# In every attention loop, the turn of a head's probabilities is issued last on TensorE, and VectorE copies the turned head before it takes the maxima

## The chip, the cores and the metric

The kernel runs on one core of a Trainium2 chip. The metric is the time of one execution on the device, in microseconds (us), taken as the median of the runs. PE or TensorE is the matmul engine, DVE or VectorE and ACT or ScalarE the two elementwise engines, SP the engine that issues the weight loads.

## What is computed

Two small transformer stages on 256 tokens of width 1024, batch 1, all in float32. The first block joins a gated linear recurrence with a three-branch attention (compressed, selected and window keys, 16 query heads on 4 key heads) and a gated feed-forward layer. The second has two layers, each an attention and a feed-forward layer: a rotary causal attention of 16 heads, and a latent attention (MLA) of 16 heads. What bears on the change is the same in all:

```python
s = jnp.einsum("bqhd,bkhd->bhqk", qi, k, preferred_element_type=jnp.float32) * scale
s = jnp.where(key_pos[None, :] <= qpos[:, None], s, NEG_INF)
p = jax.nn.softmax(s, axis=-1).astype(v.dtype)
return jnp.einsum("bhqk,bkhd->bqhd", p, v)
```

With 256 tokens the selected branch and the window branch of the first attention are both plain causal attention, so its loop runs over 32 heads (16 query heads in each of two branches), and the other two loops over 16.

## The kernel before, in words

The weights are cut in 128x1024 chunks, which go through one stream: SP loads a chunk into one of three raw buffers, ACT writes its rounded part (`split_high`, L1088, into `w_high`), DVE the rest (`split_low`, L1486, into `w_low`), and TensorE multiplies high by high, high by low and low by high (`split_product`, L531 to L537). The ring of split chunks has six places. A product of 128 outputs over a width of 1024 is 24 matmuls.

Each engine runs a program of its own, written out in order, and waits on semaphores. An attention is a loop with the same index i on three engines; head i is begun in iteration i and finished in iteration i + 3 (count + 3 iterations in all).

- TensorE, `attention` at L635. `scores(i)` (L638) makes the products of queries and keys of head i in one of three banks and adds the mask (matmuls at L644, L645, L647). `turn(i)` (L651) transposes the probabilities of head i, three 128x128 blocks, into a bank (L657). `values(i)` (L661) multiplies them with the values (L669, L670, L671); it waits until DVE has copied the turned head to SBUF. `between(i)` makes products that don't belong to this head: in the first attention half a merge gate, 12 matmuls (`merge_between`, L921; iterations 0, 1, 4 to 19, 32 and 34), in the second the turn of a rotary operand (`turn_rope`, L961, matmul at L968) and the 24 matmuls of the next query or key tile (`next_query_or_key`, L980; up to iteration 11, the turn up to 12), in the third the 9 matmuls of the query of head i + 3 (`query_product`, L1044; up to iteration 12).
- ACT, `attention` at L1153: two exponentials a head with their sums (L1161, L1163), then further work: a `split_high`, in the second attention the copy of a product (`rope_operand`, L1384), in the third the copy of a query (`query_copy`, L1445).
- DVE, `attention` at L1553. In iteration i: `before(i)` (first attention: `merge_scaled`, L1857, which reads the merge gate's bank; the next gate's first half waits for it, L882), `row_max(i)` (L1556: two reductions), `copy_turned` (L1562), every fourth iteration `output(g)` (L1568: one over the sums, and the scaled output of four heads, L1573 to L1585; in iterations 6, 10, 14, ... it waits for `values` of the same iteration of TensorE), and `after(i)`: in the first attention a `split_low`, in the second `rope(i + 3)` with a `split_low` (L1940), in the third `query_rope(i + 3)` (L2012; it reads the bank of the query product, and the product of the next head waits for it, L1050) and in six iterations a `split_low`.

The turned heads have two banks in the first and third attention and one in the second (L440, L441); their copies in SBUF have two places. After the loop `turn_output` (L686, matmuls at L696) turns the outputs, and ACT and DVE split them (`output_high`, `output_low`) for the projection. Its last pair of tiles waits for the last `output`.

Of the kernel before, what the change touches and what calls it, by code (L numbers as in the profile page):

```python
# [147 lines left out]
def build(nc, weight_stream, small_in, x_in, out):  # L148
    with ExitStack() as ctx:
# [293 lines left out]
        def of(banks, i):  # L443
            return bank[banks[i % len(banks)]]
# [83 lines left out]
        def _(pe):  # L528
# [106 lines left out]
            def attention(n, count, q, kpad, v, probs, probs_t, banks_free, before=None, between=None, use=ALL_BANKS):  # L635
                done = NH * n

                def scores(i):  # L638
                    if before:
                        before(i)  # L640
                    if i >= 3:
                        pe.wait_ge(probs_ready, done + i - 2)
                    b = of(use.scores, i)
                    mm(b[:, 0:P], q(i, 0), kpad(i)[:, 0:P], start=True, stop=False, skip_group_check=True)  # L644
                    mm(b[:, P:3 * P], q(i, 1), kpad(i), start=False, stop=False, skip_group_check=True)  # L645

                    mm(b[:, :].rearrange("p (a c) -> p a c", c=2 * P)[:, :, 0:P], ident_b[:, :],  # L647
                       mask_b[:, :].unsqueeze(1).to_broadcast([P, 2, P]), start=False, stop=True,
                       skip_group_check=True).then_inc(scores_ready, 1)

                def turn(i):  # L651
                    pe.wait_ge(probs_ready, done + i + 1)
                    ring = len(use.turned)
                    if i >= ring:
                        pe.wait_ge(probs_copied, done + i - ring + 1)
                    for j in range(3):
                        ins = nc.tensor.transpose(of(use.turned, i)[:, j * P:(j + 1) * P],  # L657
                                                  probs[:, i % 3, j * P:(j + 1) * P], ident)
                    ins.then_inc(probs_turned, 1)

                def values(i):  # L661
                    pe.wait_ge(probs_copied, done + i + 1)
                    g = i // 4
                    if i % 4 == 0 and g >= 2:
                        pe.wait_ge(o_read, 4 * n + g - 1)
                    b = of(use.outputs, g)
                    pt = probs_t[:, i % 2, :]
                    at = (i % 4) * HD
                    mm(b[:, at:at + HD], pt[:, 0:P], v(i, 0), start=True, stop=True)  # L669
                    mm(b[:, S + at:S + at + HD], pt[:, P:2 * P], v(i, 0), start=True, stop=False)  # L670
                    mm(b[:, S + at:S + at + HD], pt[:, 2 * P:3 * P], v(i, 1), start=False,  # L671
                       stop=True).then_inc(pv_done, 1)

                for i in range(count + 3):
                    if i < count:
                        scores(i)
                    if i == 2:
                        banks_free()
                    if 2 <= i < count + 2:
                        turn(i - 2)  # L680
                    if i >= 3:
                        values(i - 3)
                    if between:
                        between(i)

            def turn_output(n, o):  # L686

# [233 lines left out]
            def merge_between(i):  # L921

                if i in MG_AT:
                    at = MG_AT.index(i)
                    merge_gates(MG_EARLY + at // 2, (at % 2,))

            attention(0, 2 * NH, lambda i, t: q0[:, i % NH // 2, t * P:(t + 1) * P],
                      lambda i: k0[:, i // NH, i % 2, i % NH // 4, :],
                      lambda i, t: v0[:, i // NH, t, (i % NH // 4) * HD:(i % NH // 4 + 1) * HD], probs0, probs_t0,
# [58 lines left out]
            for n in range(1, QK_AHEAD):  # L988
                query_or_key(n)
                turn_rope(n - 1)  # L990
            pe.wait_ge(zeros_ready, 2)
            attention(2, NH, lambda h, t: q1[:, h // 2, t * P:(t + 1) * P], lambda h: k1[:, h % 2, h // 2, :],
                      lambda h, t: v1[:, t, h * HD:(h + 1) * HD], probs1, probs_t1, lambda: None,
                      lambda h: pe.wait_ge(rope_done, max(2 * (h // 2) + 2, h + 1)), next_query_or_key, SIX_BANKS)
# [77 lines left out]
            for h in range(UQ_AHEAD):  # L1072
                query_product(h)
            attention(3, NH, lambda h, t: q2[:, h, t * P:(t + 1) * P], lambda h: k2[:, h, :],
                      lambda h, t: v2[:, t, h * HD:(h + 1) * HD], probs2, probs_t2,
                      lambda: None,
# [396 lines left out]
        def _(dve):  # L1473
# [9 lines left out]
            def link(ins):  # L1483
                dve.wait_ge(dve_step, mark(ins))
# [68 lines left out]
            def attention(n, count, o, probs_t, gated=False, before=None, after=None, use=ALL_BANKS):  # L1553
                done = NH * n

                def row_max(i):  # L1556
                    dve.wait_ge(scores_ready, done + i + 1)
                    b, h = of(use.scores, i), i % NH
                    v.tensor_reduce(neg_max[:, h, 0:1], b[:, 0:P], AX.X, ALU.max, negate=True)  # L1559
                    v.tensor_reduce(neg_max[:, h, 1:2], b[:, P:3 * P], AX.X, ALU.max, negate=True).then_inc(max_ready, 1)  # L1560

                def copy_turned(i):  # L1562
                    dve.wait_ge(probs_turned, done + i + 1)
                    if i >= 2:
                        dve.wait_ge(pv_done, done + i - 1)
                    v.tensor_copy(probs_t[:, i % 2, :], of(use.turned, i)[:, 0:3 * P]).then_inc(probs_copied, 1)  # L1566

                def output(g):  # L1568

                    dve.wait_ge(pv_done, done + 4 * g + 4)  # L1570
                    heads = slice(4 * g % NH, 4 * g % NH + 4)
                    w = weights_o[:, :, heads]
                    link(v.reciprocal(w, sums[:, :, heads]))  # L1573
                    if gated:
                        link(v.tensor_tensor(w, w, nsa_gate[:, :, heads, 1 + 4 * g // NH], ALU.mult))
                    dst = o[:, :, heads, :]
                    src = of(use.outputs, g)[:, :].rearrange("p (t h d) -> p t h d", t=TT, h=4)
                    wide = w.unsqueeze(3).to_broadcast([P, TT, 4, HD])
                    if gated:
                        if 4 * g >= NH:  # L1580
                            dve.wait_ge(o_read, g - 3)
                        link(v.tensor_tensor(o_part, src, wide, ALU.mult))
                        v.tensor_tensor(dst, dst, o_part, ALU.add).then_inc(o_read, 1)
                    else:
                        v.tensor_tensor(dst, src, wide, ALU.mult).then_inc(o_read, 1)  # L1585

                for i in range(count + 3):
                    if before:
                        before(i)
                    if i < count:  # L1590
                        row_max(i)
                    if 2 <= i < count + 2:
                        copy_turned(i - 2)
                    if i >= 3 and i % 4 == 2:
                        output((i - 3) // 4)
                    if after:
                        after(i)
# [307 lines left out]
            def merge_split(i):  # L1905
                if i - 1 in MG_LATE:
                    split_low(BASE["mg"] + MG_LATE[i - 1] + RING)

            attention(0, 2 * NH, o0, probs_t0, gated=True, before=merge_gate, after=merge_split)
            merge_gate(2 * NH + 3)  # L1910
            output_low(0)
# [43 lines left out]
            for n in range(QK_AHEAD - 1):  # L1955
                rope(n)
            attention(2, NH, o1, probs_t1,
                      after=lambda i: rope(i + QK_AHEAD - 1) if i + QK_AHEAD <= SIZE["qk1"] else None, use=SIX_BANKS)
            output_low(1)
# [65 lines left out]
            def behind_maxima(i):  # L2025
                query_rope(i + UQ_AHEAD)
                query_split(i + UQ_AHEAD - 2)

            attention(3, NH, o2, probs_t2, after=behind_maxima)
            output_low(2)  # L2030
            stage("wo2", lambda i: None, count=DT - LATE)
# [188 lines left out]
```

## Time and profile before, and how to read them

| | us |
|---|---|
| median of 3 runs | 1224.09 |
| lowest and highest run | 1222.18, 1225.47 |
| the profiled execution | 1222.21 |
| its span | 1220.4 |
| TensorE busy in it | 1162.5 (95%) |
| DVE busy | 915.0 (75%) |
| ACT busy | 681.7 (56%) |
| mean granted clock of TensorE | 0.982 |

The span is the time from the first to the last instruction in the trace; the execution's own time lies 1.8 us above it. Times in the trace count from the span's start. A row of a timeline gives the start, the duration, engine, line, operation, output and inputs, the shape and how many instructions are merged; in square brackets stand the idle time before it and what ended it. Matmuls overlap, so what a matmul costs is read from start to start. The granted clock is 1.00 where TensorE runs at 2.4 GHz and 0.50 at 1.2 GHz.

The three attention loops lie at 262 to 347 us (head scores of iteration 20 at 319.68), at 632 to 702 us (iteration 12 at 689.43) and at 957 to 1001 us (iteration 13 at 990.94).

### The profile page before, as it was taken

How to read it: one execution, taken by the hardware profiler on the slowest of the kernel's cores; microseconds unless marked ns; L12 is line 12 of the kernel's file. 1: busy time of each engine (PE TensorE's matmuls, PEld its weight loads, DVE VectorE, ACT ScalarE, POOL GpSimd, SP SyncE). 2: the span in 40 equal slices, each digit the busy share in tenths (PEclk: the TensorE clock that was granted, in tenths of full speed). 3: DMA queues.
4: the chain of work that ended last, by engine and by line, in shares of the span. 5: the costliest groups of instructions: out<-in, count | busy, mean ns of one | idle time of the engine just before them, and what ended most of it. 6: DMA issues, size and time to landing. Idle time of an engine off the chain costs nothing.

```text
span 1220.4 us, 25342 instructions
## 1 busy us (share of the span) xinstructions
PE 1162.5 (95%) x9633; PEld 1132.0 (93%) x9633; DVE 915.0 (75%) x1579; ACT 681.7 (56%) x1184; POOL 9.2 (1%) x12
## 2 busy tenths in 40 slices
PE   5987998999999999999999999999998899999996
PEld 5987898999999999999899899999997899999996
DVE  6778789467777899888867758777776776777775
ACT  5755774334454666565654455655565745655552
POOL 1000000000000100000000000000000000000000
PEclk9988998999999999999999999999999999999998
DMA  6564444432216477666463325766654224576660
GB/s 222 189 209 131 147 156 130 147 121 71 70 53 190 137 224 215 200 189 192 149 194 111 98 87 193 223 194 196 192 156 149 93 70 132 187 220 201 190 190 35
DMA packets 52780, 190.82 MB, mean 156 GB/s; under 512 B 5984, under 2 KB 5984, under 8 KB 52704
## 3 DMA queue, kind: packets, MB, share of 16 engines
q1 hardware_dynamic: 52416, 188.77, 49.8%
q8 instruction: 54, 0.88, 0.3%
q10 hardware_dynamic: 288, 0.99, 0.2%
q14 instruction: 22, 0.18, 0.0%
HBM read 188.69 MB, written 1.05 MB: 155 GB/s over the span
## 4 chain that ended last, share of the span: by engine, by line
PE 82%; DVE 8%; ACT 5%; issue 2%; DMA 2%; SPq 0%; DVEq 0%; ACTq 0%
PE bank L535 23%; PE bank L537 23%; PE bank L536 23%; DVE w_low L1491 2%; DMA w_raw<-weight_stream 2%; PE bank L645 2%; ACT w_high L1096 2%; PE bank L657 1%; PE bank L671 1%; PE bank L670 1%; PE bank L644 1%; PE bank L669 1%; PE bank L543 1%; PE bank L545 1%; PE bank L544 1%
## 5 line engine op out<-in xcount | busy, mean ns | idle before, releaser
L1491 DVE TENSOR_TENSOR w_low<-w_raw,w_high 128x1024 fp32r<-128x1024 f32 x356 | 434.3, 1223 | 153.5 <-ACT w_high L1096 151.4
L1096 ACT ACTIVATE w_high<-w_raw 128x1024 fp32r<-128x1024 f32 x356 | 375.4, 1059 | 289.3 <-PE bank L537 217.9
L535 PE MATMUL bank<-h_high,w_high 128*128 128x256 f32 x1824 | 518.2, 284 | 14.7 <-DVE h_low L1529 9.7
L536 PE MATMUL bank<-h_low,w_high 128*128 128x256 f32 x1824 | 509.3, 279 | 0.0
L537 PE MATMUL bank<-h_high,w_low 128*128 128x256 f32 x1824 | 509.0, 279 | 0.0
L535 PEld LDWEIGHTS bank<-h_high,w_high 128*128 128x128 f32 x1824 | 347.0, 190 | 17.6 <-issue 12.9
L536 PEld LDWEIGHTS bank<-h_low,w_high 128*128 128x128 f32 x1824 | 347.3, 190 | 0.5
L537 PEld LDWEIGHTS bank<-h_high,w_low 128*128 128x128 f32 x1824 | 346.9, 190 | 0.0
L535 PE MATMUL bank<-r_high,w_high 128*128 128x256 f32 x878 | 248.6, 283 | 12.8 <-ACT arena L1297 7.3
L536 PE MATMUL bank<-r_low,w_high 128*128 128x256 f32 x878 | 245.4, 280 | 0.0
L537 PE MATMUL bank<-r_high,w_low 128*128 128x256 f32 x878 | 245.4, 279 | 0.0
L535 PEld LDWEIGHTS bank<-r_high,w_high 128*128 128x128 f32 x878 | 167.3, 191 | 16.9 <-ACT arena L1297 8.4
L536 PEld LDWEIGHTS bank<-r_low,w_high 128*128 128x128 f32 x878 | 167.3, 190 | 0.1
L537 PEld LDWEIGHTS bank<-r_high,w_low 128*128 128x128 f32 x878 | 167.0, 190 | 0.0
L1613 DVE SCALAR_TENSOR_TENSOR arena<-arena,small 128x255 f32<-128x255 f32 (+1 forms) x184 | 87.8, 477 | 5.7 <-ACT arena L1189 2.4
L1161 ACT ACTIVATE arena<-bank,stats 128x128 f32<-128x128 f32 x64 | 23.5, 367 | 63.3 <-DVE stats L1560 61.7
L1189 ACT ACTIVATE arena<-arena,small 128x256 f32<-128x256 f32 x68 | 40.0, 589 | 12.9 <-DVE arena L1627 12.8
L1515 DVE TENSOR_TENSOR r_low<-arena,r_high 128x256 fp32r<-128x256 f32 (+1 forms) x91 | 39.7, 437 | 5.0 <-ACT r_high L1202 4.0
L1627 DVE TENSOR_TENSOR arena<-bank,rstd 128x256 f32<-128x256 f32 x68 | 28.7, 423 | 18.1 <-PE bank L537 18.0
L1559 DVE TENSOR_REDUCE stats<-bank 128x1 f32<-128x128 f32 x64 | 18.5, 289 | 29.5 <-PE bank L647 29.2
L1566 DVE COPY arena<-bank 128x384 f32<-128x384 f32 x64 | 34.9, 548 | 4.7 <-PE bank L657 4.7
L645 PE MATMUL bank<-arena 128*128 128x256 f32 x128 | 38.3, 381 | 0.0
(205 smaller groups left out, 1164.4 us busy)
## 6 DMA issues: line engine op xcount, KB each, us to landing
w_raw<-weight_stream SPq DMA_DIRECT2D x356, 512.0 KB, 3.7
x<-x_in SPq DMA_DIRECT2D x4, 256.0 KB, 6.0
out<-arena SPq DMA_DIRECT2D x4, 256.0 KB, 2.3
small<-small_in ACTq DMA_DIRECT2D x1, 937.5 KB, 8.4
small<-small_in ACTq DMA_DIRECT2D x1, 30.0 KB, 4.0
```

The lines of the kernel that those rows point to most:

```text
L535: mm(out_ap, wh, high, start=start, stop=False, skip_group_check=True)
L536: mm(out_ap, wh, low, start=False, stop=False, skip_group_check=True)
L537: return mm(out_ap, wl, high, start=False, stop=stop, skip_group_check=True)
L645: mm(b[:, P:3 * P], q(i, 1), kpad(i), start=False, stop=False, skip_group_check=True)
L1096: fn(w_high[:, c % RING, :], w_raw[:, c % RAW, :], ACT.Copy).then_inc(high_ready, 1)
L1161: fn(probs[:, i % 3, 0:P], b[:, 0:P], ACT.Exp, bias=neg_max[:, h, 0:1], accum_out=sums[:, 0, h:h + 1])
L1189: fn(taps_g[:, j % 2, :], scaled_g[:, j % 2, :], ACT.Identity, scale=tap(f"fcw{n}", 2, k + j), bias=tap(f"fcb{n}", 0, k + j)).then_inc(tap ...
L1491: v.tensor_tensor(w_low[:, c % RING, :], w_raw[:, c % RAW, :], f(w_high[:, c % RING, :]), ALU.subtract).then_inc(low_ready, 1)
L1515: v.tensor_tensor(dst, src, f(high), ALU.subtract).then_inc(done, 1)
L1566: v.tensor_copy(probs_t[:, i % 2, :], of(use.turned, i)[:, 0:3 * P]).then_inc(probs_copied, 1)
L1613: return v.scalar_tensor_tensor(dst[:, tokens:S], src[:, 0:S - tokens], tap(row, j), dst[:, tokens:S], ALU.mult, ALU.add)
L1627: v.tensor_tensor(scaled_g[:, slot, :], bank[slot][:, 0:S], rstd[:, :], ALU.mult).then_inc(g_scaled, 1)
```

## The change

On TensorE an iteration was scores, turn, values, between; it becomes scores, between, values, turn, each with the same indices as before. On DVE the copy of a turned head was made behind the maxima of the iteration, for head i - 2; it is now made ahead of them, for head i - 3, so it stands one iteration later. Nothing is added or removed. The order in `attention` of ACT, the buffers and the wait conditions are as they were.

```diff
@@ TensorE, attention
                     if i == 2:
                         banks_free()
+                    if between:
+                        between(i)
+                    if i >= 3:
+                        values(i - 3)
                     if 2 <= i < count + 2:
                         turn(i - 2)
-                    if i >= 3:
-                        values(i - 3)
-                    if between:
-                        between(i)
@@ DVE, attention
                     if before:
                         before(i)
+                    if i >= 3:
+                        copy_turned(i - 3)
                     if i < count:
                         row_max(i)
-                    if 2 <= i < count + 2:
-                        copy_turned(i - 2)
                     if i >= 3 and i % 4 == 2:
                         output((i - 3) // 4)
```

## Rows read from the trace of the kernel before

**Rows 1.** Windows, first attention: stretch, length, busy PE, PEld, DVE, ACT, POOL, granted clock, DMA.
```profile
262.00:321.00 59.00, 59.00 (x487) 55.90 (x486) 42.14 (x95) 26.70 (x89) 0.00 (x0) 1.00 0.25 73
321.00:351.00 30.00, 28.35 (x224) 25.72 (x224) 22.37 (x57) 13.45 (x53) 0.00 (x0) 1.00 0.11 36
```

**Rows 2.** Waits of TensorE in the three attentions: us in total, times, longest.
```profile
PE bank L669 <- DVE arena L1566: 1.3, 2, 0.9
...
PE bank L657 <- DVE arena L1566: 1.6, 2, 1.2
...
PE bank L669 <- DVE arena L1566: 1.0, 1, 1.0
```

**Rows 3.** Timeline of TensorE, first attention and the start of the projection.
```profile
275.82 0.38 PE L644 MATMUL bank<-arena 128*128 128x128 f32 x2
...
319.68 0.38 PE L644 MATMUL bank<-arena 128*128 128x128 f32 x2
...
328.44 0.44 PE L669 MATMUL bank<-arena 128*128 128x64 f32 x2 [0.44 <-DVE arena L1566]
...
329.16 0.44 PE L644 MATMUL bank<-arena 128*128 128x128 f32 x2
...
329.98 0.49 PE L657 MATMUL bank<-small,arena 128*128 128x128 f32 x3
330.31 0.33 PE L669 MATMUL bank<-arena 128*128 128x64 f32 x2
...
330.92 0.44 PE L644 MATMUL bank<-arena 128*128 128x128 f32 x2
...
350.83 0.36 PE L535 MATMUL bank<-r_high,w_high 128*128 128x256 f32 x1 [0.20 <-DVE r_low L1515]
```

**Rows 4.** Timeline of DVE, first attention.
```profile
282.28 0.42 DVE L1859 TENSOR_TENSOR arena<-bank,rstd 128x256 f32<-128x256 f32 x1
...
325.54 0.19 DVE L1573 RECIPROCAL stats<-stats 128x8 f32<-128x8 f32 x1
...
327.31 0.28 DVE L1559 TENSOR_REDUCE stats<-bank 128x1 f32<-128x128 f32 x1
...
327.84 0.55 DVE L1566 COPY arena<-bank 128x384 f32<-128x384 f32 x1
...
330.18 0.29 DVE L1559 TENSOR_REDUCE stats<-bank 128x1 f32<-128x128 f32 x1 [0.80 <-PE bank L647]
```

**Rows 5.** Timeline of DVE, second attention, an iteration with an output.
```profile
661.54 0.19 DVE L1573 RECIPROCAL stats<-stats 128x8 f32<-128x8 f32 x1
...
664.04 1.23 DVE L1491 TENSOR_TENSOR w_low<-w_raw,w_high 128x1024 fp32r<-128x1024 f32 x1
```

**Rows 6.** Timeline of TensorE, second attention: scores of iteration 12, turned outputs.
```profile
689.43 0.38 PE L644 MATMUL bank<-arena 128*128 128x128 f32 x2
...
701.92 1.92 PE L696 MATMUL bank<-small,arena 128*128 128x128 f32 x16
```

**Rows 7.** Timeline of DVE, third attention, an iteration with an output.
```profile
973.46 0.20 DVE L1573 RECIPROCAL stats<-stats 128x8 f32<-128x8 f32 x1
...
974.42 0.43 DVE L2015 SCALAR_TENSOR_TENSOR arena<-bank,small 64x256 f32<-64x256 f32 x1
```

**Rows 8.** Timeline of ACT, third attention: a query's copy.
```profile
964.24 0.37 ACT L1448 ACTIVATE arena<-bank 64x256 f32<-64x256 f32 x1
```

**Rows 9.** Timeline of TensorE, third attention: scores of iteration 13, last values, turned outputs.
```profile
990.94 0.38 PE L644 MATMUL bank<-arena 128*128 128x128 f32 x2
...
999.89 0.62 PE L669 MATMUL bank<-arena 128*128 128x64 f32 x2
...
1001.15 3.02 PE L696 MATMUL bank<-small,arena 128*128 128x128 f32 x16
```

**Rows 10.** Windows, the end of the third attention, columns as in rows 1.
```profile
996.50:1000.00 3.50, 2.42 (x21) 2.04 (x21) 2.49 (x6) 0.91 (x4) 0.00 (x0) 1.00 0.38 133
1000.00:1003.40 3.40, 3.40 (x17) 3.40 (x18) 1.42 (x3) 0.89 (x2) 0.00 (x0) 0.50 0.06 22
```

## The prediction, made before the changed kernel was run

> **What bounds the kernel now.** I read the windows first. In the first attention, as long as gate products fill the gaps, TensorE is busy for all of 59.00 us; in the part without them it is busy for 28.35 of 30 [rows 1]. The waits of TensorE on the copy of a turned head come next: 1.3, 1.6 and 1.0 us in the three attentions, 3.9 in all, and no wait on the exponentials is there [rows 2]. So the loops are bound by TensorE's own issue. The change takes no work from it, and the waits that it could take away are worth 3.9 us at most. What it can do is make TensorE wait where it didn't. That is read from the timelines.
>
> **The prices.** On TensorE the scores of a head cost 0.82 us (329.16 to 329.98), its turn 0.33, its values 0.61 (330.31 to 330.92), but 0.72 when they had to wait (328.44 to 329.16), so a wait costs 0.11 beyond its length [rows 3]. A head without filler is thus 1.76. With half a gate it is (319.68 - 275.82)/14 = 3.13, so scores and half gate are 2.19 together [rows 3]. On DVE two maxima cost 0.53 and may start 0.20 after the scores (330.18 against 329.98); the copy takes 0.55, and TensorE starts 0.05 after it (328.39 to 328.44); an output of the first attention holds DVE for 1.77 (325.54 to 327.31), the read of a gate for 0.42 [rows 3, 4]. In the second attention output and rope are 2.50 together (661.54 to 664.04), a split is 1.23 [rows 5]. In the third the output is 0.96 and the query's rope 0.43 [rows 7].
>
> **What changes.** The output of an iteration waits for the values of the same iteration. Those now stand behind the filler, 0.33 ahead of the next head's scores, so the output starts 0.33 - 0.22 = 0.11 before those scores (0.2 is the way from TensorE to DVE, as for the maxima). Behind it on DVE are queued the rope or split of this iteration, then the next copy. Before, that copy was already made one iteration earlier; now the values of the next iteration need it at once. This is the step I expect to decide. I count from the start of the scores that follow an output iteration.
>
> First attention, iterations with gates. Output until 1.66, copy until 2.21, so the values start at 2.26 instead of 2.19: 0.18 with the price of the wait. Then maxima, split and gate read end near 4.3; the next gate's first half could start at 3.13 + 0.18 + 0.8 = 4.1, so 0.3 more. Four outputs (6, 10, 14, 18) with the first wait, three with the second: 1.6; the first values of the loop now wait for their copy too, 0.3. Sum **+1.9**.
>
> First attention, iterations from 20 on. The copy is done at 2.21 again but the values' place is at 0.8: 1.4 + 0.05 + 0.11 = 1.6, for outputs 22, 26 and 30: 4.8. The last two splits of the gates (iterations 20 and 21) each put a copy late by 0.9: 1.8. The last head has nothing between turn and values: 0.20 + 0.55 + 0.05 + 0.11 = 0.9. The last output comes behind the last values instead of beside half a gate's products, so the last pair of turned tiles and the projection wait 1.2. That is 8.7. What falls away are the old waits: from 319.68 to the projection at 350.83 [rows 3] are 31.15; twelve heads at 1.76, two half gates of 1.4, the last turns and values (2.5) and the sixteen turns of outputs (1.92, [rows 6]) make 28.4, which leaves 2.7. Scores behind a turn instead of behind values I put at 0.04 less, 0.5 for twelve heads. Sum 8.7 - 2.7 - 0.5 = **+5.5**.
>
> Second attention. TensorE's turn of the rope operand waits until DVE has done the rope before it, and it now stands right behind the scores. After outputs 6 and 10 the rope ends at -0.11 + 2.50 = 2.39 and is wanted at 0.8: 1.6 + 0.05 + 0.11 = 1.8 twice, 3.6. From iteration 12 on the waits are 2.0 (iteration 13, behind the last split), 0.65 (behind the output of 14), and three times 0.9 for the last three heads, where turn, copy and values are now a chain: 5.4. The old waits there: 701.92 - 689.43 = 12.49 [rows 6], less four scores, six turns, seven values and a rope turn of 0.45, together 10.0: 2.5. With 0.1 for the scores, the tail is +2.8. Sum **+6.4**.
>
> Third attention. At the start the query products stand ahead of values and turn, 0.9 earlier, while ACT copies the query before them only at 964.61 [rows 8]: 0.9. After outputs 6 and 10 the query's rope ends at -0.11 + 0.96 + 0.43 = 1.28, wanted at 0.8: 0.65 twice. Output 6 has a split behind it as well, so the copy ends at 3.1 against a place at 2.5: 0.65. The middle is 2.9. From iteration 13 on: 0.85 (split), 2.0 (output and split in iteration 14), three times 0.9, together 5.5; the old waits are 999.89 - 990.94 = 8.95 [rows 9] less three scores, five turns and five values (7.2): 1.8. With 0.1 for the scores +3.6. Sum **+6.5**.
>
> What costs nothing: ACT's and DVE's splits come up to 2 us later, but they fill a ring of six chunks, and a chunk lasts TensorE 2.8 us or more, so the weight stream and SP, which waits for those splits, keep their lead; POOL has no part. The turn's wait for the exponentials ends one product later than it needs to, and was no wait before [rows 2].
>
> Two terms have no row. The order of small and large matmuls: values behind a product, turn behind values, scores behind a turn. The two prices of the same values, 0.61 and 0.72 [rows 3], bound such a seam at 0.1 either way; over 64 heads I take the 0.04 gain counted above in the tails and nothing elsewhere, and keep -4 to +4 for the range. The clock: at the end of the third attention TensorE was busy for 2.42 of 3.50 us and then ran at 0.50, 1.2 GHz, for 3.4 us; sixteen turns took 3.02 there and 1.92 at 2.4 GHz [rows 6, 9, 10]. The new tails of the first two attentions are as thin as that (0.94 to 1.04 busy in 1.75 us per head). Each such fall costs between nothing, beside a wait, and half of 3.4 = 1.7; I take two more at 1.2 (nearest to the 1.1 of the sixteen turns): **+2.4**.
>
> The sum is 1.9 + 5.5 + 6.4 + 6.5 + 2.4 = 22.7. Against the profiled execution, 1222.2, this is 1244.9; the median of the runs stands 1.9 higher, so **1246.8**.
>
> **Rivals.** *Only the tails count.* In the stretches with filler the waits I found are 1.9 + 3.6 + 2.9 = 8.4 us, some of them small differences of long sums. If DVE gets through there in time, 12 remain of the loops, with a small clock term: 1224.1 + 12 = 1236. For it: DVE is busy for only 42 of 59 us there [rows 1]. Against: the 2.50 us of output and rope stand in one piece between two things TensorE wants [rows 5].
>
> *The clock falls often.* If TensorE falls to 1.2 GHz behind each of the waits of 1.6 us and more, some seven falls at 1.7 beside the 20.3: 1224.1 + 20.3 + 10 to 12 = 1255. For it: rows 10. Against: the 1.2 us wait of the second attention [rows 2] cost no clock, since its sixteen turns ran at full speed [rows 6].
> The Trainium skill ("Perfetto Trace Analysis", Matmul Optimizations) says that the engine scales its power with use and that matmuls should run back to back; by that rule this rival is the likelier one. The trace agrees at one place of three.
>
> *No change.* An engine that isn't the busiest hides its delays: DVE would absorb output, split and copy, 75% busy against 95%, and the time stays at 1224.
> The Trainium skill ("Perfetto Trace Analysis", Identifying the Most-Contended Engine) says to work on the engine with the highest occupancy first; by it alone a reorder on DVE would be worth nothing. The trace disagrees: TensorE waits 3.9 us on a DVE that is less busy.
>
> *Faster.* The copy stands ahead of the maxima, so values find it done. Place: the tails. Price: 3.9 us of waits gone and 0.04 for each of 64 scores, 2.6: 1224.1 - 6.5 = 1217.6. It decides this way if DVE is free 0.15 us after the scores begin (0.8 - 0.05 - 0.55 = 0.2), which needs outputs shorter than 0.3; they are 0.9 and 1.77 [rows 4, 7].
>
> **How the numbers follow.** Forecast 0.70, only the tails 0.12, clock 0.12, no change 0.03, faster 0.03. The forecast's own bounds are 20.3 - 4 and 20.3 + 4 + 3.4, so 1240 to 1252. To take in most of the two slower neighbours, 1234 to 1256. A measurement of this kernel can tell about 0.3%, 3.7 us, from no change. Faster 0.03, same 0.03, slower 0.94.
>
> **What would show it.** In the changed trace: waits of TensorE on L1566 of some 20 us instead of 3.9; waits of about 1.7 us of the rope turn (L968) on L1951 twice; in the third attention waits of the query product on L2015; head scores at 1.76 us apart broken every fourth head by 1.6; the last three heads of each loop 1.75 apart; no wait on weights that wasn't there. Wrong is the forecast if the loops keep their lengths in the filled stretches (first rival), if the granted clock shows more than four new falls (second), or if the waits on L1566 shrink.

## The result, and the profile after

The changed kernel takes 1248.2 us (median of 5 runs, 1241.84 to 1248.83) against 1223.49 for the kernel before: ratio 1.0191, 95% interval 1.0163 to 1.0219. (The ratio comes from all executions; the quotient of the two medians is 1.0202. The means are 1246.8 and 1223.4, 23.4 us apart, where the medians are 24.7 apart.) Forecast were 1246.8 us, a range of 1234 to 1256, and slower with a chance of 0.94. The profiled execution took 1241.84 us, the shortest of the five.

The span of that execution is 1240.1 us; TensorE is busy in it for 1166.3 us, as long as before but for 4 us. The waits of TensorE in the three attentions, one answer for each, in the columns of [rows 2]:

```profile
PE bank L669 <- DVE arena L1566: 5.5, 6, 1.3
PE bank L696 <- DVE arena L1583: 0.6, 1, 0.6
...
PE bank L669 <- DVE arena L1566: 4.2, 5, 1.8
PE bank L968 <- DVE arena L1951: 3.1, 2, 1.6
...
PE bank L669 <- DVE arena L1566: 4.6, 6, 1.5
...
PE bank L535 <- DVE arena L2015: 0.9, 2, 0.5
PE bank L535 <- ACT arena L1448: 0.5, 1, 0.5
```

The copies of turned heads (L1566) now keep TensorE waiting for 14.3 us instead of 3.9, and there are the waits that the forecast named: the rope turn (L968) twice on the rope (L1951), the query product (L535) twice on the query's rope (L2015) and once on ACT's copy (L1448), the last turned outputs (L696) on the last output. The forecast had named some 20 us of waits on L1566. It counted with each wait the price of 0.11 us and the way of 0.05 behind it, which the profile doesn't book as a wait, and put several of them a little too high.

A wait behind an output, in the second attention of the changed kernel, as a timeline of DVE and TensorE:

```profile
668.01 0.20 DVE L1573 RECIPROCAL stats<-stats 128x8 f32<-128x8 f32 x1 [3.25 <-PE bank L671]
668.15 0.39 PE L644 MATMUL bank<-arena 128*128 128x128 f32 x2
...
668.86 0.42 DVE L1943 TENSOR_TENSOR arena<-arena 128x256 f32<-128x256 f32 x1
...
669.64 0.85 DVE L1951 TENSOR_TENSOR arena<-arena 64x256 f32<-64x256 f32 x2
...
670.64 0.67 PE L968 MATMUL bank<-arena,small 128*128 128x256 f32 x2 [1.57 <-DVE arena L1951]
```

DVE has waited 3.25 us for the values (L671) that now stand behind the products, starts the output 0.14 us ahead of the next head's scores (L644), and reaches the end of the rope 2.5 us later. TensorE wants the rope right behind the scores. Before, this output lay beside the products. In this iteration the copy behind the rope costs nothing, since 24 products lie between the rope turn and the values.

The heads without filler show the other half. Timeline of TensorE and DVE of the changed kernel, first attention, one head far from an output, up to the next scores:

```profile
331.18 0.39 PE L644 MATMUL bank<-arena 128*128 128x128 f32 x2
...
331.38 0.56 DVE L1566 COPY arena<-bank 128x384 f32<-128x384 f32 x1 [0.48 <-PE bank L657]
...
331.99 0.43 PE L669 MATMUL bank<-arena 128*128 128x64 f32 x2
...
332.71 0.50 PE L657 MATMUL bank<-small,arena 128*128 128x128 f32 x3
...
333.04 0.39 PE L644 MATMUL bank<-arena 128*128 128x128 f32 x2
```

DVE begins the copy of the head just turned 0.20 us after these scores begin and takes 0.56; TensorE starts the values at 0.81, 0.05 behind the copy's end and later than the scores alone would let it (a turn or a product follows the mask's product after at most 0.11, here it is 0.16). A head is 1.86 us instead of 1.76 [rows 3].

Where the loops begin and end in the changed kernel (scores of iterations 0 and 20 or 12 or 13, and the first turned outputs or the projection), timeline of TensorE:

```profile
260.27 0.38 PE L644 MATMUL bank<-arena 128*128 128x128 f32 x2
319.24 0.39 PE L644 MATMUL bank<-arena 128*128 128x128 f32 x2
356.46 0.36 PE L535 MATMUL bank<-r_high,w_high 128*128 128x256 f32 x1 [0.37 <-DVE r_low L1515]
...
635.58 0.38 PE L644 MATMUL bank<-arena 128*128 128x128 f32 x2
696.45 0.39 PE L644 MATMUL bank<-arena 128*128 128x128 f32 x2
712.62 3.62 PE L696 MATMUL bank<-small,arena 128*128 128x128 f32 x16
...
967.72 0.46 PE L644 MATMUL bank<-arena 128*128 128x128 f32 x2 [2.74 <-DVE arena L2015]
1004.68 0.39 PE L644 MATMUL bank<-arena 128*128 128x128 f32 x2
1019.95 3.62 PE L696 MATMUL bank<-small,arena 128*128 128x128 f32 x16
```

From such rows comes a table for all kernels that were profiled. "Filled" is from the scores of iteration 0 to those of iteration 20 in the first attention, 12 in the second, 13 in the third; "tail" from there to the first of the sixteen turned outputs. In the kernel before, the filled parts begin at 262.27, 631.74 and 956.81, and the tails as in [rows 3, 6, 9].

| us | 1st filled | tail | 2nd filled | tail | 3rd filled | tail | sum | rest of the span |
|---|---|---|---|---|---|---|---|---|
| before | 57.41 | 29.04 | 57.69 | 12.49 | 34.13 | 10.21 | 200.97 | 1019.4 |
| after | 58.97 | 34.09 | 60.87 | 16.17 | 36.96 | 15.27 | 222.33 | 1017.8 |

The loops are 21.4 us longer; with the turned outputs behind them and the wait of the projection, 24.7 (worked out below). The rest of the span was 1.6 us shorter in this one execution.

### The profile page after: what moved, and what is told of

The parts are those of the page before. It is cut to its first block, busy times and chain, and to the rows that moved or that the text cites. A ratio compares the mean times of both kernels' runs of the same rounds, so it can differ in the third digit from the quotient of the medians.

```text
span 1240.1 us, 25342 instructions
## 1 busy us (share of the span) xinstructions
PE 1166.3 (94%) x9633; PEld 1128.5 (91%) x9633; DVE 917.8 (74%) x1579; ACT 682.6 (55%) x1184; POOL 9.2 (1%) x12
## 4 chain that ended last, share of the span: by engine, by line
PE 79%; DVE 11%; ACT 5%; issue 3%; DMA 2%; SPq 0%; DVEq 0%; ACTq 0%
PE bank L535 22%; PE bank L537 22%; PE bank L536 22%; DVE w_low L1491 3%; DMA w_raw<-weight_stream 2%; ACT w_high L1096 2%; PE bank L645 2%; PE bank L669 1%; PE bank L657 1%; PE bank L671 1%; PE bank L670 1%; DVE arena L1729 1%; DVE arena L1566 1%; PE bank L644 1%; DVE r_low L1515 1%
## 5 line engine op out<-in xcount | busy, mean ns | idle before, releaser
L535 PE MATMUL bank<-h_high,w_high 128*128 128x256 f32 x1824 | 516.1, 283 | 17.3 <-DVE h_low L1529 9.6
L535 PEld LDWEIGHTS bank<-h_high,w_high 128*128 128x128 f32 x1824 | 345.2, 189 | 25.2 <-issue 14.6
L535 PE MATMUL bank<-r_high,w_high 128*128 128x256 f32 x878 | 248.5, 283 | 12.9 <-ACT arena L1297 7.3
L535 PEld LDWEIGHTS bank<-r_high,w_high 128*128 128x128 f32 x878 | 167.6, 191 | 16.6 <-ACT arena L1297 8.3
L1161 ACT ACTIVATE arena<-bank,stats 128x128 f32<-128x128 f32 x64 | 23.5, 368 | 90.9 <-DVE stats L1560 90.7
L1566 DVE COPY arena<-bank 128x384 f32<-128x384 f32 x64 | 35.6, 556 | 33.3 <-PE bank L657 32.9
L669 PEld LDWEIGHTS bank<-arena 128*128 128x128 f32 x128 | 19.9, 194 | 23.6 <-DVE arena L1566 23.0
L669 PE MATMUL bank<-arena 128*128 128x64 f32 x128 | 25.1, 279 | 14.4 <-DVE arena L1566 14.3
```

The lines of the kernel that those rows point to most:

```text
L535: mm(out_ap, wh, high, start=start, stop=False, skip_group_check=True)
```

## The experiments

All ratios are to the kernel before, run beside them on the same chip. Where a kernel's lines are shifted, the text says which operation a line is.

**1. The changed kernel again.** No edit. The forecast stood 22.7 us above the kernel before and the profiled execution 19.6, the median 24.7.

> The changed kernel once more, with a profile of its own, because its profiled execution (1241.84 us) lies 6 us under its other runs. Theory of the late output: the waits in the three loops are the same to 0.1 us in every execution (21 us in all), and what differs between 1242 and 1248 lies elsewhere or in the clock. Rival, the clock: the slower executions have more stretches at 1.2 GHz inside the attentions. Expected median 1247, ratio 1.018 to 1.020.

Measured: median 1245.05 us (1239.73 to 1248.92), ratio 1.0190, interval 1.0167 to 1.0212. The waits are the same to 0.1 us: 14.3, 3.1, 0.9 and 0.5. The loops: 58.98, 34.05, 60.88, 16.97, 36.99, 15.69, together 223.56; the rest 1020.6, 2.8 us more than in the first profile. So the filled parts repeat to 0.03 us in these two profiles; what moves from one to the other are the tails of the second and third attention and the rest of the span. The rival, the clock, is not out: of the changed kernel's ten executions the four with a mean granted clock of 0.979 or more took 1239.73 to 1245.98 us, the six below it 1245.05 to 1248.92. The kernel before does the same: in the last series of experiment 6, its executions at 0.984 or more took 1218.27 to 1221.70 us, those at 0.980 or less 1223.82 to 1225.36. Where in an execution without a profile the clock fell isn't known. In the profiled execution of this series the clock fell earlier, inside the second tail, and was back before the sixteen turns. Windows, in the columns of [rows 1], and the turns:

```profile
700.00:703.40 3.40, 1.56 (x13) 1.15 (x11) 3.32 (x8) 0.91 (x4) 0.00 (x0) 1.00 0.35 141
703.40:706.80 3.40, 3.40 (x17) 3.03 (x17) 1.09 (x4) 0.91 (x4) 0.00 (x0) 0.55 0.48 154
```
```profile
715.35 1.92 PE L696 MATMUL bank<-small,arena 128*128 128x128 f32 x16
```

**2. The new order in one part of the loops only.** `late` is 20 in the first attention and 12 in the others. For the tail alone the condition is turned round; DVE then leaves out the copy in iteration `late`, which is already made. The bounds on the first and last heads are left out in the diff.

```diff
@@ TensorE, filled part alone
+                    if i < late:
+                        between(i)
+                        values(i - 3)
+                        turn(i - 2)
+                    else:
                         turn(i - 2)
                         values(i - 3)
                         between(i)
@@ DVE, filled part alone
+                    if i <= late:
+                        copy_turned(i - 3)
                     if i < count:
                         row_max(i)
-                    if 2 <= i < count + 2:
+                    if late <= i < count + 2:
                         copy_turned(i - 2)
```

> The new order on both engines only in the iterations with filler products (0 to 19 in the first attention, 0 to 11 in the others), the old order behind them. Theory of the late output: only the mid-loop waits of the changed kernel remain, 1.6 + 3.2 + 2.8 = 7.6 us, so 1231 us, ratio 1.006. Rival (only the chain turn, copy, values in the heads without filler costs): under 1 us, 1224. Rival (clock): 1231 plus 2 to 4.

Measured: 1231.22 us, ratio 1.0076 (1.0062 to 1.0089). Loops 59.10, 29.49, 60.86, 12.68, 38.32, 9.67, together 210.12.

> The old order in the iterations with filler, the new one behind them (from 20 and 12 on). Theory of the late output: only the tails' extra waits remain, 6.1 + 3.7 + 5.1 = 14.9 us by the changed kernel's trace, 14 of them without its clock, so 1238 us, ratio 1.012. The parts add up: this and the filled part alone give the whole change, some 22. Rival (the parts don't add, because the late DVE of the filled part is what makes the tail late): under 10.

Measured: 1235.34 us, ratio 1.0115 (1.0096 to 1.0134). Loops 57.48, 33.60, 57.70, 15.47, 34.18, 15.82, together 214.25. The filled parts are those of the kernel before to 0.1 us, the tails those of the changed kernel to 0.7.

Against the kernel before the two are 9.6 and 13.7 us longer, together 23.4, and the whole change is 23.5 in the same series: the parts add, and the rival by which only the tails count is out. The tails came out as forecast (14), and the filled part is 2.0 above its 7.6. Most of that is the clock. The third attention's filled part is 38.32 us here and 36.96 in the changed kernel, and 1.25 of the difference lies in its first four iterations, where the clock fell: windows of the filled kernel, then of the changed one, columns of [rows 1].

```profile
962.87:974.10 11.23, 10.57 (x69) 9.43 (x70) 6.43 (x16) 6.61 (x23) 0.00 (x0) 0.85 0.32 95
```
```profile
967.72:977.70 9.98, 9.35 (x69) 8.03 (x70) 6.42 (x16) 6.42 (x23) 0.00 (x0) 1.00 0.34 107
```

The same fall, 0.85 over these iterations, stands in the profiles of the kernels of experiments 3, 4 (TensorE's half) and 5, and in no other of the twelve.

The second attention is the cleanest: its filled part is 60.86 here and 57.70 in the tail's kernel, both at a clock of 1.00.

The waits of TensorE on the rope (in the filled kernel L977 on L1965) and on the query's rope (L535 on L2029) are there in the filled kernel alone:

```profile
PE bank L977 <- DVE arena L1965: 3.1, 2, 1.6
PE bank L657 <- DVE arena L1575: 1.6, 2, 1.2
...
PE bank L535 <- DVE arena L2029: 0.9, 2, 0.5
```

The second line, L657 on the copies, is the old tail's wait of [rows 2], back at its 1.6.

**3. The output two iterations later.**

```diff
-                    if i >= 3 and i % 4 == 2:
-                        output((i - 3) // 4)
+                    if i >= 8 and i % 4 == 0:
+                        output(i // 4 - 2)
+                    if i == count + 2:
+                        output(count // 4 - 1)
```

> The changed kernel, with the output of four heads two iterations later on DVE (iterations 8, 12, ..., the last one at the end), so that it never waits for values of the same iteration. Theory of the late output: the mid-loop waits go, nearly all of the first attention's 1.6, the 3.2 of the second and half of the third's 2.8; the tails stay; 6 us less than the changed kernel, 1241, ratio 1.014. In the trace no wait of the rope turn L968 on L1951 and none of the query product on L2015. Rival (the chain turn, copy, values costs everywhere, whatever the output does): 1247 as the changed kernel, with the same waits on L1566.

Measured: 1231.76 us, ratio 1.0083 (1.0064 to 1.0103). Loops 57.12, 32.45, 57.37, 18.42, 35.98, 12.77, together 214.11. No wait of the rope turn and none of the query product on DVE is left. In the first attention, DVE's timeline in an iteration with an output:

```profile
281.85 0.56 DVE L1566 COPY arena<-bank 128x384 f32<-128x384 f32 x1 [0.24 <-PE bank L657]
...
282.82 0.41 DVE L1560 TENSOR_REDUCE stats<-bank 128x1 f32<-128x256 f32 x1
283.15 0.19 DVE L1573 RECIPROCAL stats<-stats 128x8 f32<-128x8 f32 x1
...
284.31 0.69 DVE L1583 TENSOR_TENSOR arena<-arena 128x512 f32<-128x512 f32 x1
284.94 0.56 DVE L1566 COPY arena<-bank 128x384 f32<-128x384 f32 x1
```

The output starts right behind the maxima, not behind the values, and the next copy follows it at once and in time. With the output out of the way the filled parts of the first and second attention are 0.3 us shorter than before the change, although turn and copy stand in the new order. The third is 1.85 longer than before the change, and more than that lies in its first four iterations (11.19 against 8.99): 1.2 is the fall of the clock named in experiment 2 (9.96 in the changed kernel), the rest the early query products with their wait on ACT's copy, 0.66 here. From there to the scores of iteration 13 it takes 24.79 against 25.14 before. So in the filled parts, behind their first iterations, it is the output's wait that costs, not the order as such; the rival named in the expectation is out. The size was forecast too small, 6 us against 13 measured between the medians. Of the difference of the loops' sums, 9.45 (223.56 less 214.11), 6.4 is in the filled parts, as far as expected; 1.6 and 2.9 come from the first and third tail. This third tail ran at a clock of 1.00, and some 2.4 of the 2.9 are the clock: an estimate from the 2.0 us that the last heads lost to it in the changed kernel's first profile ("The clock", below) and the 0.4 by which the tail is longer in the second. In the second tail 1.5 is lost. There the output now stands in iteration 12, and the next copy is queued behind output, rope and split and comes late by more than any copy of the changed kernel; around this wait and behind it the clock was at 0.77 on average. Timeline of TensorE, and the window:

```profile
696.71 0.69 PE L669 MATMUL bank<-arena 128*128 128x64 f32 x2 [2.68 <-DVE arena L1566]
```
```profile
693.00:711.00 18.00, 13.37 (x78) 11.68 (x77) 9.98 (x23) 3.83 (x16) 0.00 (x0) 0.77 0.10 32
```

The rest of the span is 1018.2 here and 1020.6 in the changed kernel's second profile, both within what the twelve profiles show whatever the kernel (1017.8 to 1021.6).

**4. One engine's half of the change alone.**

The first kernel takes the first part of the diff of the change, the second takes the second:

```diff
@@ TensorE, the first kernel
+                    between(i)
+                    values(i - 3)
                     turn(i - 2)
-                    values(i - 3)
-                    between(i)
@@ DVE, the second kernel
+                    copy_turned(i - 3)
                     row_max(i)
-                    copy_turned(i - 2)
```

> Only TensorE's order is changed; DVE copies the head of two iterations back behind the maxima, as before. Theory of the late output (what decides is the order of DVE's queue against the turn, which is now last): DVE now waits in every iteration for the turn at its end before it can begin output, rope or split, so the second attention's rope turn waits 1.6 us in each of 12 iterations (+19 and the outputs), the third's query product 0.55 in each and 1.4 behind outputs (+7), the first's gate 1.7 every second iteration (+13), the tails some +10: 1270 us, ratio 1.040. Rival (DVE's half of the change is what costs, TensorE's order alone is harmless): 1222 to 1226.

Measured: 1275.81 us, ratio 1.0451 (1.0433 to 1.0469). Loops 67.93, 31.67, 76.06, 17.17, 43.87, 15.42. The filled parts grow by 10.5, 18.4 and 9.7; expected were 13, 19 and 7 (of the 9.7, 1.2 is the clock's fall of experiment 2). The waits of TensorE, the first line from the first attention, the next two from the second, the last from the third:

```profile
PE bank L535 <- DVE arena L1859: 9.0, 7, 1.4
...
PE bank L968 <- DVE arena L1951: 9.3, 5, 2.4
PE bank L968 <- DVE arena L1947: 5.8, 6, 1.1
...
PE bank L535 <- DVE arena L2015: 5.3, 8, 1.4
```

The first of these waits on the rope, 0.3 us, stands in every kernel; the other ten are new, where the changed kernel has two. With DVE's old order every rope, gate read and query's rope waits behind a copy whose turn is now the last thing TensorE does. DVE's half of the change is what keeps TensorE's half from costing more than twice as much: its copy comes one iteration later, but nothing else waits behind it for the turn.

> Only DVE's order is changed; TensorE as before (scores, turn, values, products). By the hand sum: a copy now stands behind the split or output of the iteration before it and its values are wanted 1.15 us after the scores begin; the third attention waits 1.4 in six split iterations and 0.2 in the others (+9), the second hardly (+1), the first 2 with gates and 4 without, tails +2: 1240 us, ratio 1.015. Rival (TensorE's half is what costs, the copy's place is harmless): 1222 to 1226.

Measured: 1242.16 us, ratio 1.0179 (1.0160 to 1.0197). Loops 60.77, 32.27, 58.79, 16.12, 41.23, 11.38. The filled parts grow by 3.4, 1.1 and 7.1; expected were 2, 1 and 9. Both rivals, by which one half is harmless, are out: each half alone costs, TensorE's 54.7 us and DVE's 21.0, and both together 23.5.

**5. The products last.** DVE as in the changed kernel; on TensorE:

```diff
-                    between(i)
                     values(i - 3)
                     turn(i - 2)
+                    between(i)
```

> The changed kernel, with the filler products last on TensorE (scores, values, turn, products). Theory of the late output: the values are wanted 0.8 us after the scores begin, so each copy behind a split or a gate read is late: third attention 1.7 in six iterations and 0.5 in six (+13), first +4 with gates, tails as in the changed kernel (+14), second's rope waits gone: 1252 us, ratio 1.026. Rival (the turn's place behind the products is what makes output and copy late, so this is better than the changed kernel): 1235 to 1240.

Measured: 1254.87 us, ratio 1.0276 (1.0258 to 1.0294). Loops 62.83, 34.78, 57.70, 17.48, 47.19, 15.33. The second attention's filled part is back at the 57.7 of before, the first's is 5.4 longer (expected 4), the third's 13.1. That the third is as long as forecast is in part luck: TensorE waits 6.8 us there in eight waits, three of them of 1.60, 7.7 us with the price of 0.11 each, and the mean granted clock of the stretch was 0.89, where it was 1.00 before the change. So here the clock did fall more than once in the loop. A split there, and what follows, as a timeline of TensorE and DVE:

```profile
996.16 0.38 PE L644 MATMUL bank<-arena 128*128 128x128 f32 x2
...
996.81 1.23 DVE L1491 TENSOR_TENSOR w_low<-w_raw,w_high 128x1024 fp32r<-128x1024 f32 x1
998.07 0.56 DVE L1566 COPY arena<-bank 128x384 f32<-128x384 f32 x1
...
998.68 0.43 PE L669 MATMUL bank<-arena 128*128 128x64 f32 x2 [1.60 <-DVE arena L1566]
```

The values could follow the scores 0.8 us after 996.16, near 997.0, and the copy that the values need ends at 998.63. The products ahead of the values, in the changed kernel, were a cover for just this.

**6. A hybrid, and the kernel before against itself.** From iteration 4 to the end of the filler the new order, with outputs in iterations 8, 12, 16, 20 (first attention) or 7 and 11; the old order elsewhere.

```diff
+                    if 4 <= i < late:
+                        between(i)
+                        values(i - 3)
+                        turn(i - 2)
+                    else:
                         turn(i - 2)
                         values(i - 3)
                         between(i)
...
+                    if gated and 8 <= i <= late and i % 4 == 0:
+                        output(i // 4 - 2)
+                    if not gated and 7 <= i < late and i % 4 == 3:
+                        output(i // 4 - 1)
```

> What the runs before point to: the new order only from iteration 4 to the end of the filler products, with the outputs one iteration later (two in the first attention), the old order before and behind. Theory of the late output: no wait left in the filled part, and the seams save 0.04 us a head as in the kernel with the later output (57.12 against 57.41 and 57.37 against 57.69 us up to the heads without filler): 0.9 us under the kernel before, ratio 0.9985 to 1.000, not to be told from no change. Rival (a new wait at the change from one order to the other): 2 us or more above the kernel before.

Measured: 1224.03 us, ratio 1.0019 (1.0009 to 1.0029). Loops 56.78, 30.06, 57.62, 12.67, 34.01, 9.67, together 200.81. The filled parts have no new wait and are 0.6, 0.1 and 0.1 us shorter, nearly the 0.9 that was forecast, but the tail of the first attention is 1.0 us longer. Its iterations 22 and 23 take 2.11 and 2.13 us instead of 1.77 and 1.76, and the wait on the copy behind them is 0.73 instead of 0.44; that this comes from the two outputs in iterations 20 and 22, which stand close together, is likely and wasn't tested. The ratio said slower, the loops said the same.

> The kernel before against itself, with a second profile. Both theories: ratio 1.000 with an interval within 0.1% or so, and the three loops at 200.97 us as in the first profile, to 0.2 us. If the interval leaves out 1.000, ratios of 0.2% say nothing here.

Measured: ratio 0.9999 (0.9984 to 1.0013); loops 57.52, 29.02, 57.61, 12.50, 34.19, 9.68, together 200.52, which is 0.45 below the first profile and more than the 0.2 expected. The third tail makes it: 9.68 instead of 10.21, and sixteen turns of 1.92 behind it instead of 3.02. The fall of the clock that the first profile had there isn't in this one. So it comes and goes in one and the same kernel.

> The hybrid once more. Its loops took 200.81 us against 200.97, but its ratio was 1.0019. Theory of the late output (nothing but the loops differs, the rest was chance or the clock): ratio 0.998 to 1.001. Rival (something outside the loops, set off by the other code or the other phase, costs 2 us): 1.002 again, and the part outside the loops at 1021 us against 1019.4.

Measured: 1222.8 us, ratio 0.9997 (0.9983 to 1.0012); loops together 200.76. So the 1.0019 didn't repeat, and the hybrid is no version that beats the kernel before. A difference of 0.2% isn't to be told from none in this kernel by one series.

## Why the prediction was right

**What decides.** That the output, queued behind the values of its own iteration, is late and delays rope, gate read and copy behind it, is shown: with the output two iterations later those waits are gone (experiment 3), with the new order in the filled part alone they are there with the old tail behind them (experiment 2). Waits on the copy in the tails, where turn, copy and values stand as a chain, stay in experiment 3, and with the old order there they are back at 1.3, 1.6 and 1.1 us (experiment 2).

**The terms**, against the two first profiles:

| | forecast | measured |
|---|---|---|
| first attention, filled | +1.9 | 58.97 - 57.41 = +1.6 |
| first, from iteration 20 to the projection | +5.5 | 37.22 - 31.15 = +6.1 |
| second, filled | +3.6 | +3.2 |
| second, tail | +2.8 | +3.7, of it 0.7 the clock |
| third, filled | +2.9 | +2.8 |
| third, tail | +3.6 | +5.1, of it 1.5 the clock |
| clock, behind the tails | in the 2.4 below | 1.7 + 0.6 |
| clock in all, from the rows above | +2.4 | 0.7 + 1.5 + 1.7 + 0.6 = 4.5 |
| all but the clock | +20.3 | +20.2 |
| sum | 22.7 | 24.7 |

That the sum is the difference of the medians, 24.7, is chance. It comes from one execution, whose span is only 19.7 us longer, since the part before, between and behind the attentions was 5.0 us shorter in it, 2.0 of them ahead of the first scores (260.27 against 262.27). The same terms from the second profile of the changed kernel make 24.2, and the means of the executions differ by 23.4 and 23.3 us in the two series. No term but the clock is off by more than 0.6, and the agreement of 20.3 with 20.2 owes something to errors that cancel (the first tail 0.6 too small, the filled parts together 0.8 too large). The forecast that the rest of the span doesn't change is right on the mean: over the twelve profiles of this study it was between 1017.8 and 1021.6, whatever the kernel.

**Terms mis-sized.** The clock is the one that matters (next paragraph). The seam was put at a gain of 0.04 per head and taken in the tail of the first attention, 0.5 in all. In the filled parts the gain is there: a head with half a gate is 3.09 us instead of 3.13, and the row that shows where is the mask's product (L647) beside a gate product. Timeline of TensorE, after, then before:

```profile
290.74 0.27 PE L647 MATMUL bank<-mask_b,ident_b 128*128 128x256 bf16 x1
290.77 0.37 PE L535 MATMUL bank<-h_high,w_high 128*128 128x256 f32 x1
```
```profile
279.60 0.27 PE L647 MATMUL bank<-mask_b,ident_b 128*128 128x256 bf16 x1
279.71 0.49 PE L657 MATMUL bank<-small,arena 128*128 128x128 f32 x3
```

0.03 us from the mask to a gate product against 0.11 to a turn. But in the tail it is a loss: 1.86 against 1.76. The forecast had the copy done at 0.20 + 0.55 + 0.05 = 0.80 and the values due at 0.8, and so counted nothing for it; it is late by 0.05, and the price of a wait, 0.11, is then paid for every head. For the seven heads without a longer wait that is 0.14 each, 1.0 us; the whole tail came out 0.6 above its forecast, so something else in it was put 0.4 too high. It is the two copies behind the last splits, 0.9 each in the forecast: the two heads with these waits (0.48 and 0.45 us in the trace) take 2.47 and 2.43 us, 0.7 more than 1.76.

**The clock.** The forecast took two more falls at 1.2, and the number was right and the size half of it. There was one new one in the second attention, worth 0.7 + 1.7 = 2.4, and a longer one in the third, worth 1.5 + 0.6 = 2.1 more than the one before the change. Windows of the changed kernel, columns of [rows 1]:

```profile
705.30:708.70 3.40, 2.43 (x18) 1.96 (x18) 1.33 (x4) 0.91 (x4) 0.00 (x0) 1.00 0.00 0
...
712.10:715.50 3.40, 3.40 (x18) 3.40 (x18) 1.88 (x4) 1.27 (x3) 0.00 (x0) 0.50 0.00 0
...
1009.00:1012.40 3.40, 1.88 (x16) 1.47 (x14) 3.02 (x6) 1.12 (x5) 0.00 (x0) 1.00 0.04 10
...
1015.80:1022.60 6.80, 6.15 (x28) 5.75 (x29) 2.21 (x5) 1.20 (x2) 0.00 (x0) 0.50 0.00 0
```

Ahead of the two falls TensorE had been busy for 0.71 and 0.55 of the time, in turns and values of single heads with waits between them. Sixteen turns took 3.62 us in both places, against 1.92 and 3.02 before [rows 6, 9], so 2.3 more. The values and turns ahead of them took 0.7 more in the second attention and 2.0 in the third: from the last values to the first turned output 1.33 us instead of 0.72, and a head before them up to 2.84 instead of 1.86. The kernel before had lost 0.5 there itself (10.21 against 9.68 in its second profile), so 1.5 remain. The first attention kept its 1.00 in both profiles although its waits of 1.3 us are nearly as long. So for the changed kernel the rival of many falls is out as to their number: two places, not seven.

Both lie in the thin last heads. With the old order there (the filled part alone, experiment 2) neither is left: its sixteen turns took 1.92 us in both places. But the tails' kernel, with the same thin heads, kept 1.00 in the second attention (tail 15.47, turns 1.91) and fell in the third, and the kernel before fell in the third in one of its two profiles. So the thin heads go with the falls and don't fix them; what decides in one execution is open.

**The rivals.** "Only the tails count" was out by experiment 2, where the filled parts alone cost 9.6 us. "No change" and "faster" are out by the result. The rule of the Trainium skill ("Perfetto Trace Analysis", Identifying the Most-Contended Engine), to optimize the engine of the highest occupancy first, doesn't point at the order of DVE if it is taken alone: DVE is at 75% and TensorE at 95%, and the change is worth 1.9%. The harm showed as idle time of TensorE, the busiest engine, that DVE ended. An average of an engine over a loop doesn't say when its next instruction is wanted.

## What to carry to other kernels

When three engines share a loop, write down for one iteration when each result is done and when it is wanted, counted from the same instruction, and look at the iteration that carries extra work (here every fourth, with the output); the slack before it is what a reorder spends. With the outputs out of the way (experiment 3), the same copy one iteration later cost nothing where products of 1.1 us or more stood ahead of its consumer; in the changed kernel it cost 0.1 us a head and 1.5 an output where only 0.8 us of scores did. An order on two engines is one decision: each half of this change alone was 21 and 55 us slower, both together 23.5.

## What the runs showed that I had not expected

A product of the mask in bfloat16 (128x256) is followed by a product of split weights after 0.03 us, but by a transpose after 0.11. And a wait that is short in itself, 0.05 us, makes the next values 0.11 us longer each time (0.72 instead of 0.61): a loop that just misses its slot loses three times what it misses, 0.16 us a head here, of which 0.06 is gained back elsewhere in the head. And the same kernel's time goes with its mean granted clock, by some 7 us between 0.980 and 0.987 in the kernel before (1225.36 and 1218.27 us), so a difference of a few us between two executions needs the clock beside it.
